# Sums over channels in four column groups, and the memory's keys multiplied by token

## The reference

```python
def conformer_conv_branch(a_glu, gate, dw, dw_b, ln_g, ln_b, w_proj):
    a, b = jnp.split(a_glu, 2, axis=-1)
    u = a * jax.nn.sigmoid(b)
    u = lax.conv_general_dilated(u, dw[:, None, :], window_strides=(1,), padding=[(CONV_K - 1, 0)], ...) + dw_b   # 31 taps, each channel by itself
    u = layer_norm(u, ln_g, ln_b)              # mean and variance over 1024 channels
    u = jax.nn.silu(u) * jax.nn.silu(gate)
    return u @ w_proj

def memory_cross_attention_branch(q, gate, mem_h, w_mem_kv, qn_g, kn_g, w_proj):
    k, v = jnp.split(mem_h @ w_mem_kv, 2, axis=-1)         # 256 memory tokens
    q = rms_norm(q.reshape(B, S, X_HEADS, X_HEAD_DIM), qn_g)   # 4 heads of 256 features
    k = rms_norm(k.reshape(B, M, X_HEADS, X_HEAD_DIM), kn_g)
    v = v.reshape(B, M, X_HEADS, X_HEAD_DIM)
    s = jnp.einsum("bshd,bmhd->bhsm", q, k) * (X_HEAD_DIM ** -0.5)
    o = jnp.einsum("bhsm,bmhd->bshd", softmax(s), v).reshape(B, S, X_WIDTH) * jax.nn.silu(gate)
    return o @ w_proj

def first_block(...):
    h, mem_h = rms_norm(x, norm_g[l]), rms_norm(mem, mem_norm_g[l])
    (c_glu, c_gate, d_q, d_k, d_v, d_gate, x_q, x_gate, merge) = jnp.split(h @ w_in[l], IN_SPLITS, axis=-1)
    g = jax.nn.sigmoid(merge.reshape(B, S, N_BRANCH, D))
    y = g[:, :, 0] * y_conv + g[:, :, 1] * y_diff + g[:, :, 2] * y_mem
    x = x + y @ w_out[l]
```

## Time and profile before

| | |
|---|---|
| median of 3 runs | 1691.04 us (1688.78 to 2245.79) |
| profiled execution | 1690.89 us |
| its span in the trace | 1689.2 us |
| TensorE busy | 1603.5 us (95%) |
| VectorE busy | 996.7 us (59%) |
| ScalarE busy | 725.1 us (43%) |
| GpSimd busy | 190.2 us (11%) |
| granted TensorE clock, mean | 0.988 of full |

### The profile page before, as it was taken

One profiled execution on the slowest core, in us unless ns is written; L12 is line 12 of the kernel. 1 busy time (PEld: TensorE's weight loads), 2 busy tenths in 40 slices (PEclk: granted clock), 3 DMA queues, 4 the chain that ended last, 5 costly groups with the idle time before them and its releaser, 6 DMA issues. The chain is left out here.

```text
span 1689.2 us, 24321 instructions
## 1 busy us (share of the span) xinstructions
PE 1603.5 (95%) x9944; PEld 1263.7 (75%) x9944; DVE 996.7 (59%) x1676; ACT 725.1 (43%) x1155; POOL 190.2 (11%) x158
## 2 busy tenths in 40 slices
PE   6999989999999999899999899989998999999997
PEld 5776876788878776677778787767766787888886
DVE  4999975456655477647444747776546453334445
ACT  6533347335522467647632525545423332232212
POOL 2433445400010000000004100000000000000000
PEclk9999999999999999999999999999999999999999
DMA  5222234444455322222234232210002332323231
GB/s 204 88 88 87 78 110 125 162 162 149 133 171 174 118 82 88 77 99 74 82 119 144 63 119 75 75 39 4 3 26 76 107 118 87 95 93 97 91 100 50
DMA packets 45645, 166.07 MB, mean 98 GB/s; under 512 B 5264, under 2 KB 5392, under 8 KB 45536
## 3 DMA queue, kind: packets, MB, share of 16 engines
q1 hardware_dynamic: 42912, 155.95, 28.8%
q0 software_dynamic: 2624, 8.59, 1.7%
HBM read 162.42 MB, written 2.10 MB: 97 GB/s over the span
## 5 line engine op out<-in xcount | busy, mean ns | idle before, releaser
L569 PE MATMUL bank<-h_T_hi,weight_hi 128*128 128x512 f32 x1208 | 496.2, 411 | 5.0 <-DVE h_T_lo L2085 2.8
L604 ACT ACTIVATE weight_hi<-raw 128x1024 fp32r<-128x1024 f32 x241 | 254.9, 1057 | 559.4 <-PE bank L571 553.4
L612 DVE TENSOR_TENSOR weight_lo<-raw,weight_hi 128x1024 fp32r<-128x1024 f32 x184 | 225.5, 1225 | 443.4 <-ACT weight_hi L604 443.4
L570 PE MATMUL bank<-h_T_lo,weight_hi 128*128 128x512 f32 x1208 | 480.2, 398 | 0.0
L571 PE MATMUL bank<-h_T_hi,weight_lo 128*128 128x512 f32 x1208 | 480.1, 397 | 0.0
L569 PEld LDWEIGHTS bank<-h_T_hi,weight_hi 128*128 128x128 f32 x1208 | 229.1, 190 | 66.8 <-issue 11.7
L570 PEld LDWEIGHTS bank<-h_T_lo,weight_hi 128*128 128x128 f32 x1208 | 229.3, 190 | 56.3 <-issue 5.6
L571 PEld LDWEIGHTS bank<-h_T_hi,weight_lo 128*128 128x128 f32 x1208 | 228.6, 189 | 55.6
L2080 DVE SCALAR_TENSOR_TENSOR bank<-conv_in,columns,bank 128x512 f32<-128x512 f32 x240 | 181.4, 756 | 8.3
L612 POOL TENSOR_TENSOR weight_lo<-raw,weight_hi 128x1024 fp32r<-128x1024 f32 x57 | 138.6, 2437 | 200.5 <-ACT weight_hi L604 200.4
L569 PE MATMUL bank<-branch_hi,weight_hi 128*128 128x512 f32 x192 | 76.0, 396 | 1.4 <-DVE scratch_more L2080 1.4
(11 more groups left out here) (448 smaller groups left out, 2320.8 us busy)
## 6 DMA issues: line engine op xcount, KB each, us to landing
raw<-in_weights SPq DMA_DIRECT2D x289, 512.0 KB, 3.5
x_in<-in_x SPq DMA_DIRECT2D x4, 512.0 KB, 5.7
x_rows<-in_x POOLq DMA_DIRECT2D x4, 512.0 KB, 4.9
out<-x_rows SPq DMA_DIRECT2D x4, 512.0 KB, 2.6
mem_in<-in_mem POOLq DMA_DIRECT2D x2, 512.0 KB, 8.4
ln_rows<-in_ln_g POOLq DMA_DIRECT2D x4, 256.0 KB, 3.8
ln_rows<-in_ln_b POOLq DMA_DIRECT2D x4, 256.0 KB, 4.5
silu_row<-in_c POOLq DMA_DIRECT2D x1, 512.0 KB, 11.4
```

What stands on the lines that cost most here:

```text
L569: pe.matmul(o, lhs[0], rhs[0], start=start, stop=False)
L570: pe.matmul(o, lhs[0], rhs[1], start=False, stop=False)
L604: act.activation(parts[n % SPLIT][0][:, :], raw[u % RAW][:, :], ACT.Copy).then_inc(*weight_hi.up(u))
L612: engine.tensor_tensor(lo[:, :], raw[u % RAW][:, :], view(hi[:, :]), ALU.subtract).then_inc(*ready.up(u))
```

## The change

1. **Sums in column groups.** The sums over channels, for the mean and for the squares, are taken for four tiles at once. Each of four float32 products has a matrix of ones with 32 columns and writes its own group of 32 lanes of one bank; the second four add to the first. ScalarE copies the bank to SBUF (`parts_out`), and one product with a matrix of 1/32 (`mean_of_32`) adds the four groups and spreads the sum over all lanes. The eight products of the mean become two groups and one product, and so do those of the squares.
2. **Later in the order.** The mean's first group stands where the sum of tile 3 stood, the second behind the second value unit, the total behind the third. The squares' groups stand behind the first and second unit of the second half of the values, their total behind the third.
3. **Keys by token.** The keys become token units (half 0 before the gate unit of tile 7, half 1 behind its merge unit). ScalarE squares them with a sum along the row, so the products with ones are gone; VectorE scales rows by their root (`dve_key_rows`), TensorE turns them with the identity (`pe_key_turn`), and the gain is multiplied in when the high and low parts are taken.
4. **Order of ScalarE and VectorE.** The splits, the values' parts, and the loading of the exponential table stand at other places (below), and the squares have five buffers in place of three.

```diff
+    def pe_conv_parts(pe, what, bank, tiles, ready, g):
+        for j in range(4):
+            pe.wait_ge(*ready.at(4 * g + j))
+        for j in range(4):
+            done = pe.matmul(bank[cut(j, 32), :], ones_all[:, 0:32], tiles(4 * g + j), start=g == 0, stop=g == 1)
+        done.then_inc(*conv_parts.up(what, g))
+
+    def pe_conv_total(pe, what, bank):
+        pe.wait_ge(*conv_parts_out.at(what))
+        return pe.matmul(bank, mean_of_32[:, :], conv_r_ring[what], start=True, stop=True)
...
     def pe_conv_mean(pe, n):
-        pe.wait_ge(*conv_done.at(n))
-        done = pe.matmul(bank, ones_all[:, :], conv[:, n, :], start=n == 0, stop=n == KT - 1)
+        if n % 4 == 3:
+            bank = stats.take(pe, "mean", conv_normed, KT - 1) if n == 3 else stats["mean"]
+            pe_conv_parts(pe, "mean", bank, lambda i: conv[:, i, :], conv_done, n // 4)
...
+    def pe_key_turn(pe, half):
+        for t in range(MT):
+            pe.wait_ge(*key_rows.at(half, t))
+        for h in (2 * half, 2 * half + 1):
+            key_places.take(pe, ("xk turned", h), norm_lo, "xk", h, 1)
+            for c in range(2):
+                for t in range(MT):
+                    done = pe.transpose(key_turned_bank(h, c)[:, cut(t)], norm_ring["xk", half, t][:, cut(2 * (h % 2) + c)], ident[:, :])
+            done.then_inc(*key_turned.up(h))
...
     def pe_keys(pe):
-        pe_key_units(pe, 2)
-        pe_key_units(pe, 3, mid=lambda: pe_conv_mean(pe, KT - 1))
-        pe_key_sum(pe, 2)
+        for pair in range(KT // 2):
+            pe_key_pair(pe, 1, pair, out_banks)
+            if pair == 0:
+                pe_key_turn(pe, 0)
+        pe.wait_ge(*conv_done.at(KT - 2))
...
-                for n in range(3 * pair, min(3 * pair + 3, KT)) if half == 0 else ():
-                    pe_conv_squares(pe, n)
+                if half == 0 and pair == 1:
+                    pe_key_turn(pe, 1)
+                    pe_conv_mean(pe, KT - 1)
+                if half == 0 and pair == 2:
+                    pe_conv_total(pe, "mean", stats["mean"]).then_inc(*conv_mean.up())
+                if half == 1 and pair < 2:
+                    pe_conv_squares(pe, pair)
+                if half == 1 and pair == 2:
+                    pe_conv_total(pe, "squares", square_places["conv_sq"]).then_inc(*conv_summed.up())
...
-            if n == KT - 1 and j == 14:
-                dve_key_full(dve, 0)
-            if n == KT - 1 and j == 18:
+            if n == KT - 1 and j == 4:
+                dve_key_rows(dve, 0)
+            if n == KT - 1 and j == 20:
                 dve_key_lo(dve, 0)
...
+    def dve_key_rows(dve, half):
+        dve.wait_ge(*key_rooted.at(half))
```

182 lines of the change are left out of this document (87 added, 95 removed).

## The result

The changed kernel takes **1662.58 us** (median; 1661.95 to 1663.21 in five runs), the kernel before 1690.24 beside it: ratio 0.9837, interval 0.9824 to 0.9851. Of the five runs of the kernel before, four lie between 1688.47 and 1691.04, and one took 2245.79, which no run here explains. The gain is 28 us, where 10.7 were forecast. The order of events behind the forecast came out nearly as written. The error is elsewhere: about half of the gain comes from a line of the diff that was never priced.

What follows compares the result with a forecast made beforehand. TensorE, busy 95% of the span, was taken as the bound, alternating with VectorE in 140 to 311 us. Projection 0 13.9 us earlier, less 3.2 for the clock, gave 1690.9 - 10.7 = 1680.2 us; over 8 in 10 for 1675 to 1687.

Steps and rivals of the forecast that it cites:

- (f): From projection 0 to the end: 13.9 us less 3.2 for the clock leaves 10.7, carried to the end, 1680.2.
- clock charge: TensorE's clock falling after two new waits, of 3.2 and 5.4 us: 1.6 us lost for each, 3.2 together.
- (a): TensorE up to tile 7 of the convolution: conv_b starts at 190.6, where it was 194.3 before.
- (b): Keys of half 0 and VectorE's tile 7: keys done 213.0, no VectorE wait, last tap 243.4, 1.9 us later.
- (c): Up to the mean's total: new 3.2 us wait before half 1's turned keys, total done 250.7, mean not earlier.
- (d): From the mean to the norm's root: squares' total done at 264.8, root at 266.2 against 272.03 before.
- (e): From root to projection 0: ScalarE's loop ends 287.5, query sum waits 5.4 us, projection 0 at 297.2, 13.9 earlier.
- rival 5: VectorE's new wait behind tap 4 of tile 7 delays everything, making the change slower: 1692 or so; chance 0.04.
- rival 4: The clock doesn't fall in the two new waits: 1677, or 1675 with the loop tighter; chance 0.11.
- The group's price: Four float32 products in four column groups run beside each other on TensorE, 1.0 us, judged from the second block's quadrant products.
- rival 2: The four column groups go one behind the other on TensorE, 3.6 us each: 1686; chance 0.14.
- Rival 3: ScalarE's in-order queue before projection 0 is longer than counted: 1681.5 to 1685, or 1687 with query squares delayed; chance 0.11.

Runs made afterwards that it cites:

- the third run of the first group: The changed kernel with `small` at 384 columns in place of 376, so h_T is back at 96 past a multiple of 128 bytes: 1676.28 us.
- plain sums: Changed kernel at the good address, sums as full-width products adding in PSUM in place of column groups, no copy or total: 1651.36 us.
- plain-sum kernel at the changed kernel's own address: Changed kernel with its own layout, sums as full-width products adding in PSUM in place of column groups, no copy or total: 1667.35 us.

## Why the prediction was wrong

**The step that failed is the last of (f): "Everything behind 311 waits for TensorE or moves with it, so I carry the 10.7 us to the end."** It assumes that a product costs the same in both kernels. The diff has `small` growing; neither the account of the change above nor the prediction mentions it, and 0.233 us was used for the changed kernel as for the old one. That line alone is worth 10 us on the kernel before, and undone in the changed kernel it costs 13.7 (1676.3 against 1662.6). A second term was mis-sized: the clock charge of 3.2 us, of which nothing reached projection 0. With both put right the forecast is 10.7 + 3.2 + 13.7 = 27.6 us, beside 27.7 measured. The prediction's own last sentence named the sign (the gain at projection 0 isn't the gain at the end), but gave no mechanism for it.

**The order's own gain was right.** Before its clock charge the chain gives 13.9 us at projection 0; at equal addresses it is 14.1 to 14.6. The fair test of the steps is the changed kernel at the old address (the third run of the first group), since the prediction used the old distance:

| | forecast | old address | as given |
|---|---|---|---|
| (a) conv_b of tile 7 starts | 190.6 | 190.89 | 189.58 |
| (b) keys of half 0 done | 213.0 | 213.42 | 213.48 |
| (b) VectorE begins tile 7 | 215.09 | 215.41 | 214.10 |
| (b) its last tap ends | 243.4 | 243.6 | 242.3 |
| (c) wait before the turned keys | 3.2 | 2.78 | 1.47 |
| (c) mean's second group starts | 246.0 | 246.29 | 244.99 |
| (c) mean's total starts | 249.8 | 250.20 | 248.89 |
| (d) total of the squares starts | 263.9 | 264.67 | 263.32 |
| (e) ScalarE's loop ends | 287.5 | 286.7 | 285.3 |
| (e) waits behind it | 5.4 | 1.91 | 1.93 and 0.87 |
| (e) projection 0 | 297.2 | 296.53 | 294.68 |

- (b) There is no wait of VectorE in tile 7, so rival 5 had nothing to stand on. That the tile begins a microsecond earlier in the kernel as given comes with the address.
- (c) The mean is indeed hardly earlier (centring 249.95 for 250.69).
- (e) One query wait of 5.4 us was forecast. The same queue on ScalarE was met one unit earlier, before x_gate 1, for a bank that ScalarE empties behind the branch, and little was left of it at the query's sum. The two are smaller than forecast since ScalarE was through sooner and TensorE there later. That the sum still comes out within a microsecond is in part such errors cancelling.
- (f) **The clock charge of 3.2 us was not due.** Windows of TensorE in the changed kernel (busy time with products, then the granted clock):

```profile
131.00:134.00 3.00, 1.85 (x7) 0.68 0.00 0
188.00:191.00 3.00, 1.42 (x4) 0.85 0.00 0
200.00:286.00 86.00, 82.60 (x368) 1.00 0.40 126
286.00:290.00 4.00, 3.13 (x13) 1.00 0.15 61
```

The clock fell behind the waits of 3.09 at 132 and 3.20 at 189.6, and behind none of the later, shorter ones. The second fall made the keys of half 0 take 23.9 us (189.58 to 213.48) in place of 22.4, and that went into the wait before the turned keys. At the old address the clock did fall behind one of the two new waits, the one of 1.91 us, where behind the 1.93 of the kernel as given it did not:

```profile
287.20 0.50 PE L569 MATMUL bank<-h_T_hi,weight_hi 128*128 128x512 f32 x1 [1.91 <-ACT scratch L580]
```

```profile
286.00:295.00 9.00, 7.79 (x23) 0.81 0.36 116
```

There TensorE reached the query's sum at 291.39, when ScalarE's squares were ending (291.45), so this fall too cost nothing at projection 0. Wrong in (f) is to put the charge on the chain: the time that the clock took stood before waits for another engine. And the length of a wait alone doesn't tell whether the clock falls. Without the charge the forecast would have been 1677, rival 4's number and within 1 us of 1676.28, the changed kernel at the old address.

**The group's price was right**, within 0.1 us: 1.00 us to the next start four times, 1.10 by the prediction's measure, so rival 2 falls. Its reading of the quadrant rows holds for column groups too. The rule that it set against them, from the Trainium skill ("TensorE: Matmul & The Clock Gate", Part 3), is that a weight load overlaps running products only where its row group differs. It doesn't hold for four column groups in float32 here: 1.10 us against 3.44 at full width. The prediction's estimate of 1.3 to 1.5 us was too high as well. TensorE's row of weight loads shows the group's eight together, as its products start:

```profile
244.99 0.16 PEld L891 LDWEIGHTS bank<-conv_out,ones_all 128*32 128x32 f32 x8 [0.17 <-issue]
```

But the prediction took the groups to be a source of the gain beside the order. They are worth 0.6 to 3.0 us with the new order and cost 4 us or more without it. The rest of the change, which is the new places, the keys by token and the new order on ScalarE and VectorE, carries 11 to 13.5 of the 14 us (308.88 to 297.72, and 309.19 to 295.69). How these three share it is not separated by any run.

Rival 3 didn't show: ScalarE's loop ended before the 287.5 of the forecast.

## What to carry to other kernels

Read a diff for its allocations as well as its instructions: a buffer that grows by 96 bytes moves every operand placed behind it, and where one engine is full for 95% of the span, 3% on the distance of its instructions (24 us) outweighs the whole change under study (14 us). Compare two versions only with their operands at the same distance from each other, or try both at each; here the best kernel is neither of the two given, but the new order with plain sums and h_T and weights both at multiples of 128 bytes, 1651.4 us. And a saving of engine time (8 us of products for the groups) is worth only what doesn't fall into waits that the other engines impose.

## What the runs showed that was not expected

- The distance between two products of 512 columns on the short parts (`mm3`) depends on where the moving operand starts against the loaded one: 0.2268 us with a difference that is a multiple of 128 bytes, 0.2289 or 0.2333 at 64 (by which of the two moves), 0.2333 at 96. Moving both by the same amount changes nothing (1690.6 beside 1691.0, 1666.4 beside 1665.3).
- In the changed kernel the feature units between 202 and 286 us kept 0.2333, though their addresses are those of the others; they follow token units without a wait of TensorE between. From 286 on they had 0.2289. Following token units isn't enough for it: in the kernel before with 376 columns the feature units from 283.5, and in the plain-sum kernel at the changed kernel's own address those from 272.9, do so too and had 0.2289. No run shows why; at a difference of 0 it doesn't occur.
- Four float32 products in four column groups take little more than the time of one: 1.10 us, where one takes 0.87 and four at full width 3.44.
- Whether the clock falls behind a wait differs between kernels with the same instructions: not behind 1.93 us before x_gate 1 in the changed kernel, but behind 1.91 us at the same place with h_T 32 bytes on (0.81 of full in the 9 us around it).
